# Expert weights as the stationary operand in full fp32, in place of three split fp32r products

## The reference, cut to what matters

```
def _expert_choice_ffn(h, p):
    cap = CAPACITY_FACTOR * S // N_EXPERTS            # 64 latent tokens, 16 context tokens
    aff = softmax(h @ p['w_router'] + p['b_router'])
    gate, idx = lax.top_k(aff.transpose(0, 2, 1), cap)
    xs = h[idx]                                        # the tokens of each expert
    gg, uu = xs @ w_e_gate[e], xs @ w_e_up[e]          # 1024 x 1024 each
    y = (silu(gg) * uu) @ w_e_down[e] * gate           # 1024 x 1024
    return zeros.at[idx].add(y)
```

## Time and profile before

| what | us |
|---|---|
| median of 2 runs (1469.69 to 1471.41) | 1470.55 |
| the profiled execution's own time | 1475.51 |
| its span, first to last instruction | 1473.7 |
| PE busy (share of the span) | 1327.3 (90%) |
| PEld busy | 1068.4 (72%) |
| DVE busy | 969.6 (66%) |
| ACT busy | 666.8 (45%) |
| POOL busy | 319.2 (22%) |
| HBM bytes read | 286.63 MB |

### The profile page before, as it was taken

How to read it: one execution, slowest core, us unless ns; L and a number is a source line. 1 busy time by engine, 2 the same in 40 slices (tenths; PEclk the granted TensorE clock), 3 DMA queues, 4 the chain that set the end, 5 groups by cost and what they waited for, 6 DMA issues and landing times.

```text
span 1473.7 us, 18979 instructions
## 1 busy us (share of the span) xinstructions
PE 1327.3 (90%) x7386; PEld 1068.4 (72%) x7386; DVE 969.6 (66%) x1083; ACT 666.8 (45%) x718; POOL 319.2 (22%) x199
## 2 busy tenths in 40 slices
PE   4699998899689999999979846999999999999992
PEld 3488787799568889999979734666666666666661
DVE  5443345467896643261365464999999999999993
ACT  3642232222233431241321224777777777777772
POOL 0211132000022222232322130222222222222212
PEclk9688799999799999999999757999999999999997
DMA  9645244112210112112520396999999999999974
GB/s 288 220 127 187 86 128 87 58 58 83 90 42 17 43 48 68 58 58 87 203 85 30 131 383 214 353 379 383 384 383 383 384 382 382 382 381 375 378 254 151
DMA packets 155867, 302.55 MB, mean 205 GB/s; under 512 B 6810, under 2 KB 60501, under 8 KB 155552
## 3 DMA queue, kind: packets, MB, share of 16 engines
q1 hardware_dynamic: 144268, 267.89, 50.6%
q0 software_dynamic: 3760, 12.45, 4.1%
q10 hardware_dynamic: 7782, 21.40, 4.0%
HBM read 286.63 MB, written 15.08 MB: 205 GB/s over the span
## 4 chain that ended last, share of the span: by engine, by line
PE 81%; DVE 10%; ACT 3%; DMA 2%; issue 2%; SPq 1%; POOL 0%; ACTq 0%; POOLq 0%; DVEq 0%
PE bank L1270 15%; PE bank L1271 14%; PE bank L1272 14%; PE bank L1293 5%; PE bank L1296 4%; PE bank L1294 4%; PE bank L1295 4%; PE bank L1297 4%; PE bank L1298 4%; DVE fa L899 2%; PE bank L1495 1%; PE bank L1329 1%; PE bank L1568 1%; PE bank L1330 1%; DMA wring<-in_w_ada 1%
## 5 line engine op out<-in xcount | busy, mean ns | idle before, releaser
L1202 DVE TENSOR_TENSOR l2r<-w,h2r 128x2048 fp32r<-128x2048 f32 x189 | 431.6, 2290 | 55.5 <-ACT h2r L806 53.7
L806 ACT CAST h2r<-w 128x2048 fp32r<-128x2048 f32 x192 | 367.1, 1913 | 131.4 <-PE bank L1272 128.5
L1270 PE MATMUL bank<-h2r,xTh 128*80 128x512 f32 x512 | 203.5, 397 | 1.0 <-DVE xTl L1208 1.0
L1271 PE MATMUL bank<-l2r,xTh 128*80 128x512 f32 x512 | 202.4, 395 | 0.0
L1272 PE MATMUL bank<-h2r,xTl 128*80 128x512 f32 x512 | 200.6, 392 | 0.0
L433 POOL TENSOR_TENSOR lring<-wring,hring 128x2048 fp32r<-128x2048 f32 x23 | 107.3, 4668 | 222.0 <-ACT hring L530 222.0
L489 POOL TENSOR_TENSOR half<-half 1x1 f32<-1x1 f32 x32 | 67.6, 2113 | 369.0 <-DVE ye L1246 367.7
L530 ACT CAST hring<-wring 128x2048 fp32r<-128x2048 f32 x39 | 74.3, 1907 | 104.6 <-PE bank L1298 59.0
L899 DVE SCALAR_TENSOR_TENSOR fa<-fa,cwT 128x655 f32<-128x655 f32 x120 | 110.3, 983 | 0.0
L1272 PEld LDWEIGHTS bank<-h2r,xTl 128*80 128x80 f32 x512 | 76.3, 149 | 43.2 <-issue 0.9
L1293 PE MATMUL bank<-hTh,hring 128*128 128x320 f32 x304 | 103.0, 339 | 5.0 <-DVE lring L883 5.0
(11 more groups left out here) (274 smaller groups left out, 2771.8 us busy)
## 6 DMA issues: line engine op xcount, KB each, us to landing
w<-in_w_e_gate SPq DMA_DIRECT2D x64, 1024.0 KB, 13.7
w<-in_w_e_up SPq DMA_DIRECT2D x64, 1024.0 KB, 13.8
w<-in_w_e_down SPq DMA_DIRECT2D x64, 1024.0 KB, 12.8
wring<-in_w_in SPq DMA_DIRECT2D x20, 1024.0 KB, 5.2
wring<-in_w_ada SPq DMA_DIRECT2D x12, 1024.0 KB, 6.3
fa<-in_w_ada SPq DMA_DIRECT2D x12, 1024.0 KB, 5.8
fa<-in_w_in SPq DMA_DIRECT2D x4, 1024.0 KB, 5.6
wring<-in_w_out SPq DMA_DIRECT2D x4, 1024.0 KB, 5.3
```

Of the source, the lines that this page charges most:

```text
L806: act.copy(h2r[:, k % 3, :], w2[:, k, :]).then_inc(e_hi, 1)
L1202: dve.tensor_tensor(l2r[:, k % 3, :], w2[:, k, :], h2r[:, k % 3, :].bitcast(F32), ALU.subtract).then_inc(e_lo, 1)
L1270: pe.matmul(out, lh, rh, start=start, stop=False)
L1271: pe.matmul(out, lh, rl, start=False, stop=False)
```

## The change

The weights are no longer split. A unit is now 256 rows by all 1024 columns of any of the three matrices. PE takes each 128 x 128 block of the raw fp32 unit as the stationary operand and moves the 80 token columns (`xT2` or `hT2`, fp32) past it. A unit is 8 column blocks by 2 row blocks, 16 plain fp32 matmuls. The result comes out feature-major (features on partitions, tokens along the row), so that the gated product needs no turn before `down`, but the result of `down` does: ACT copies it to `yT2` (`y_out`) and PE turns it back (`turn_back`, 8 transposes with 128 moving columns), behind the first unit of the next expert. `w2` becomes a ring of 16 units, freed by `e_unit`; SP sends 13 early, and the other three after the second norm (`s_h2`). SiLU, product and copies work on 128 x 320 tiles in place of 80 x 512. The loops are written out for all 16 experts. Gate and up units are read as two neighbouring rows per partition (8 KB in one piece), and `turn_tokens` takes every second column of `xe` to match.

```diff
-            w2 = place(p2, "w2", [P, 12, UN])
-            h2r = place(p2, "h2r", [P, 3, UN], F32R)
-            l2r = place(p2, "l2r", [P, 3, UN], F32R)
+            w2 = place(p2, "w2", [P, RING, UN])
...
-            xTh = place(p2, "xTh", [P, DC, M_E], F32R)
-            xTl = place(p2, "xTl", [P, DC, M_E], F32R)
...
+            xT2 = place(p2, "xT2", [P, DC, M_E])
+            hT2 = place(p2, "hT2", [P, DC, M_E])
+            yT2 = place(p2, "yT2", [P, DC, M_E])
...
+            for n in range(N_E * E_N):
+                e, (name, r) = n // N_E, EXPERT_UNITS[n % N_E]
+                src = a[name][0, e, 256 * r:256 * r + 256, :]
+                if n == EARLY_SLOTS:
+                    sp.wait_ge(s_h2, TT)
+                if n >= RING:
+                    sp.wait_ge(e_unit, n - RING + 1)
...
-            for k in range(3):
-                gp.wait_ge(e_hi, k + 1)
-                gp.tensor_tensor(l2r[:, k, :], w2[:, k, :], h2r[:, k, :].bitcast(F32), ALU.subtract).then_inc(e_lo, 1)
...
+            def y_out(e):
+
+                for hf in range(2):
+                    if hf == 0:
+                        act.wait_ge(e_down, e + 1)
+                    else:
+                        act.wait_ge(e_unit, N_E * e + N_E)
+                    act.copy(yT2[:, 4 * hf:4 * hf + 4, :],
+                             bank[4 + hf][:, 0:4 * M_E].rearrange("p (c t) -> p c t", c=4)).then_inc(e_yt, 1)
...
+            for e in range(E_N):
+                silu(e)
+                if e < E_N - 1:
+                    x_out(e + 1)
+                y_out(e)
...
+            def weigh(e):
+
+                if e >= 1:
+                    dve.wait_ge(e_add, 16 * e)
                 for hf in range(2):
+                    dve.wait_ge(e_yb, 2 * e + (hf + 1))
                     x = slice(512 * hf, 512 * hf + 512)
-                    dve.scalar_tensor_tensor(ye[:, x], bank[4 + hf][0:M_E, :], gateT[:, at(e)], g2r[:, x], ALU.mult,
+                    dve.scalar_tensor_tensor(ye[:, x], bank[2 + hf][0:M_E, :], gateT[:, at(e)], g2r[:, x], ALU.mult,
...
+            for e in range(E_N):
+                gated(e)
+                weigh(e)
...
+            def expert_unit(e, k):
+
+                n = N_E * e + k
+                r = k % 4
+                pe.wait_ge(e_w[n % RING], 16 * (n // RING + 1))
+                w = w2[:, n % RING, :].rearrange("p (c n) -> p c n", c=2)
+                x = hT2 if k >= 8 else xT2
+                for j in range(DC):
+                    out = bank[2 * (k // 4) + j // 4][:, M_E * (j % 4):M_E * (j % 4) + M_E]
+                    for c in range(2):
+                        last = pe.matmul(out, w[:, c, j * P:(j + 1) * P], x[:, 2 * r + c, :], start=r == 0 and c == 0 and j % 4 == 0,
+                                         stop=r == 3 and c == 1 and j % 4 == 3)
+                    if j == 3 and k == 7:
+                        last.then_inc(e_up, 1)
+                    if j == 3 and k == 11:
+                        last.then_inc(e_down, 1)
                 last.then_inc(e_unit, 1)
...
+            def turn_back(e):
+
+                for hf in range(2):
+                    pe.wait_ge(e_yt, 2 * e + (hf + 1))
+                    for c in range(4):
+                        last = pe.transpose(bank[2 + hf][0:M_E, c * P:(c + 1) * P], yT2[:, 4 * hf + c, :], ident[:, :])
+                    last.then_inc(e_yb, 1)
+
+            turn_tokens(0)
+            for e in range(E_N):
+                pe.wait_ge(e_xh, 2 * e + 2)
+                expert_unit(e, 0)
+                if e >= 1:
+                    turn_back(e - 1)
+                for k in range(1, 4):
+                    expert_unit(e, k)
+                if e >= 1:
                     pe.wait_ge(e_y, 2 * e)
+                for k in range(4, 8):
+                    expert_unit(e, k)
+                if e < E_N - 1:
+                    turn_tokens(e + 1)
+                for k in range(8, 12):
+                    if k % 2 == 0:
+                        pe.wait_ge(e_h, 2 * e + (k - 6) // 2)
+                    expert_unit(e, k)
+            turn_back(E_N - 1)
```

More of the change, by code:

```diff
@@ L96, in freed @@
     return dve, sum((JOBS[i][0] in BY_DVE) == dve for i in range(n + 1))
[L100 to L110, removed]
+EXPERT_UNITS = [("w_e_gate", r) for r in range(4)] + [("w_e_up", r) for r in range(4)]
+EXPERT_UNITS += [("w_e_down", r) for r in range(4)]
+N_E = len(EXPERT_UNITS)
+RING = 16
+EARLY_SLOTS = 13
 ITEMS = [(-1, h) for h in range(H)] + [(n, h) for n in range(4) for h in range(H)]
@@ L259, in trunk @@
         with ExitStack() as p2:
-            w2 = place(p2, "w2", [P, 12, UN])
-            h2r = place(p2, "h2r", [P, 3, UN], F32R)
-            l2r = place(p2, "l2r", [P, 3, UN], F32R)
+            w2 = place(p2, "w2", [P, RING, UN])
             xe = place(p2, "xe", [M_E, D])
-            xTh = place(p2, "xTh", [P, DC, M_E], F32R)
-            xTl = place(p2, "xTl", [P, DC, M_E], F32R)
-            sg = place(p2, "sg", [M_E, D])
-            hTh2 = place(p2, "hTh2", [P, DC, M_E], F32R)
-            hTl2 = place(p2, "hTl2", [P, DC, M_E], F32R)
+            xT2 = place(p2, "xT2", [P, DC, M_E])
+            hT2 = place(p2, "hT2", [P, DC, M_E])
+            yT2 = place(p2, "yT2", [P, DC, M_E])
             ye = place(p2, "ye", [M_E, D])
@@ L307, in trunk @@
         s_route = sem("s_route"); s_va = sem("s_va"); s_gm = sem("s_gm"); s_a2 = sem("s_a2"); s_xp = sem("s_xp"); s_u0 = sem("s_u0"); s_aa = sem("s_aa"); s_pa = sem("s_pa")
[L308 to L311, removed]
+        e_w = [sem(f"e_w{i}") for i in range(RING)]; s_bc2 = sem("s_bc2")
+        e_unit = sem("e_unit"); e_up = sem("e_up"); e_down = sem("e_down")
+        e_col = sem("e_col"); e_x = sem("e_x"); e_xt = sem("e_xt"); e_xh = sem("e_xh")
+        e_sg = sem("e_sg"); e_h = sem("e_h"); e_yt = sem("e_yt"); e_yb = sem("e_yb")
         e_y = sem("e_y"); e_cs = sem("e_cs"); e_add = sem("e_add"); s_g2 = sem("s_g2")
@@ L398, in _ @@
             unit_used(sp, N_U - 1)
[L400 to L410, removed]
+            for n in range(N_E * E_N):
[5 more added lines that the diff above has]
+                    sp.wait_ge(e_unit, n - RING + 1)
+                if name == "w_e_down":
+                    sp.dma_start(w2[:, n % RING, :].rearrange("p (c n) -> p c n", c=2),
+                                 src.rearrange("(c p) n -> p c n", p=P)).then_inc(e_w[n % RING], 16)
+                else:
+                    sp.dma_start(w2[:, n % RING, :], src.rearrange("(p c) n -> p (c n)", c=2)).then_inc(e_w[n % RING], 16)
         @block.gpsimd
@@ L497, in _ @@
             gather(0)
-            def expert(e, last):
-                if not last:
+            for e in range(E_N):
+                if e < E_N - 1:
                     gp.wait_ge(e_xt, 2 * e + 2)
                     gather(e + 1)
-                if not (isinstance(e, int) and e == 0):
+                if e >= 1:
                     gp.wait_ge(e_add, 16 * e)
@@ L510, in expert @@
                                       compute_op=ALU.add).then_inc(e_add, 16)
[L512 to L515, removed]
             for t in range(TT):
@@ L800, in _, with x_out @@
             act.dma_start(g2r[CAP_S:M_E, :], mods_d[0:1, 3 * D:4 * D].to_broadcast([CAP_P, D])).then_inc(s_g2, 16)
[L802 to L808, removed]
+            def x_out(n):
                 for hf in range(2):
                     act.wait_ge(e_xt, 2 * n + (hf + 1))
-                    act.copy(xTh[:, 4 * hf:4 * hf + 4, :],
+                    act.copy(xT2[:, 4 * hf:4 * hf + 4, :],
@@ L813, in x_hi @@
                              bank[6 + hf][:, 0:4 * M_E].rearrange("p (c t) -> p c t", c=4)).then_inc(e_xh, 1)
[L815 to L844, removed]
@@ L846, in _, with silu @@
-            for k in range(3):
-                e_hi_unit(0, k)
-            softmax_exp(TT - 1)
[L849 to L854, removed]
+            def silu(e):
+                act.wait_ge(e_unit, N_E * e + 4)
+                for hf in range(2):
+                    act.activation(hT2[:, 4 * hf:4 * hf + 4, :], bank[hf][:, 0:4 * M_E].rearrange("p (c t) -> p c t", c=4),
+                                   ACT.Silu).then_inc(e_sg, 1)
@@ new lines, in y_out @@
+            def y_out(e):
+                for hf in range(2):
+                    if hf == 0:
+                        act.wait_ge(e_down, e + 1)
+                    else:
+                        act.wait_ge(e_unit, N_E * e + N_E)
+                    act.copy(yT2[:, 4 * hf:4 * hf + 4, :],
+                             bank[4 + hf][:, 0:4 * M_E].rearrange("p (c t) -> p c t", c=4)).then_inc(e_yt, 1)
+            softmax_exp(TT - 1)
+            x_out(0)
+            for e in range(E_N):
[3 more added lines that the diff above has]
+                y_out(e)
@@ L1223, in expert, with gated @@
[L1223 to L1242, removed]
+            def gated(e):
+                for hf in range(2):
+                    if hf == 0:
```

(92 more changed lines are left out.)

17 lines of the change are left out of this document (removed).

## The result

The changed kernel takes 1679.7 us (median of 2 runs, 1678.75 to 1680.66) against 1470.55: ratio 1.142, 95% interval 1.139 to 1.145. The forecast was 1675.

The account below looks back on a forecast made before the run. TensorE was taken to bound the expert stage, DMA close behind. To 1470.6 us came +162 for pairs and turns at 2.4 GHz and +44 for the low clock: 1676, taken as 1675; range 1620 to 1800.

Parts of the forecast that it names:

- The bound: Expert stage: TensorE sets its time, DMA's floor 41 us under; taking work from DVE and ACT alone gains nothing.
- Price of a pair: Expert matmuls: weight load sets 0.1125 us a pair at 2.4 GHz, 80 columns hidden; 6144 pairs, 691.2 us.
- Turns: Expert stage, 15 of each: turn_tokens 0.55 us each, 8.3 in all; turn_back 8 x 0.11 each, 13.2 in all.
- The clock: Expert stage: 1.2 GHz through expert 0, 2.4 from its turn_back on; +44 us, chance 0.37.
- a later one: Expert stage: the clock rises only at a later turn_back burst, 41 us more an expert: 1716, 1757, 1798; chance 0.26.
- rival B: Expert stage: the clock never reaches 2.4 GHz, 2283 us; chance 0.16.
- rival C: Expert stage: the matmul stream alone raises the clock to 2.4 GHz within the first units, 1636 us; chance 0.15.
- Rival D: Expert matmuls: loads at the transposes' pace, 0.07 us a pair, DMA the bound, stage about 470 us, total 1390; chance 0.04.
- Zero prices: Expert stage: SiLU, product, copies and SP's longer queue lie beside PE's work and cost nothing.
- The sum: Expert stage: +162 us at 2.4 GHz plus 44 for the low clock, +206 in all.
- The end: Expert stage's end: ACT's last copy and 4 transposes come ahead of the second half of ye, +0.7 us.
- the token split: Expert stage's start: the split of the tokens on DVE falls away, so PE may start earlier, -0.5 us.

Follow-up runs that it names:

- e3: Changed kernel with token columns zero-padded so that 128 columns move in place of 80: 1636.4 us, ratio 1.113 to the kernel before.
- e4: Changed kernel loading only 64 of each block's 128 weight columns, half of the output features left out: 1427.0 us, ratio 0.970 to the kernel before.
- e1: Changed kernel with the 8 turn-back transposes placed singly between matmuls of units 1 and 2 of the next expert, not as one burst: 2263.8 us.
- e2: Changed kernel with 16 extra identity transposes, into a bank nobody reads, behind the first unit of expert 0: 1641.0 us.
- e7: Changed kernel with 22 matmuls of 384 fp32r columns on constants before the expert stage, during the gather: 1676.1 us, ratio 1.140 to the kernel before.
- e10: Changed kernel with gate and up units laid out like down units, so token turns load neighbouring columns: 1676.2 us, ratio 1.139 to the kernel before.
- e5: Changed kernel moving only 40 of the 80 token columns, half of the products left out: 2267.6 us.
- e8: Changed kernel with 34 warming matmuls during the gather and 6 behind the first tokens' turns: 1634.6 us, ratio 1.111 to the kernel before.
- e6: Kernel before the change with 22 warming matmuls on constants ahead of its expert stage: 1469.1 us, ratio 1.000.
- e9: Kernel before the change with 30 warming matmuls ahead of its expert stage and 6 more behind the tokens' turns: 1467.8 us, ratio 0.9986.

## Why the prediction was right

- **The bound.** TensorE set the stage before and after; the empty DVE and ACT gave nothing back. Right.
- **Price of a pair.** I took 0.1125 from plain fp32 streams with 1 and 16 columns and argued that 80 would hide behind the load. Measured 0.1115; and 128 columns (e3) and 64 loaded ones (e4) show that it is the load. At 1.2 GHz I took 0.215; 32 pairs from 976.33 to 983.15 are 0.213.
- **Turns.** `turn_back` took 0.88 us, as costed. `turn_tokens` was mis-sized, 0.94 us for 0.55, 6 us in all: the row that I took it from loads neighbouring columns, the change every second one. The cheaper pairs (6144 x 0.001 = 6 us) hid it in the sum.
- **The clock.** Cold through expert 0, up at its `turn_back`, held to the end: as forecast, near 985 us, and e1 and e2 show the burst to be the cause. This was the weakest step: it had 0.37, and that the first burst would do it, not a later one (0.26), was a guess on which 41 us hung. It was no luck of one run: the ten runs of the kernels that spend expert 0 at 1.2 GHz and keep the burst where it was (the changed kernel, e7, e10) all lie between 1672 and 1681 us, with no 1716 among them. In e5 the same burst failed, so the rise could have failed; I could not have excluded rival B, which e1 and e5 then showed in full (2264 and 2268 us against the 2283 that I gave it), nor rival C (1636), whose time e2, e3 and e8 reached by other ways (1641, 1636, 1635).
- **Rival D** needed loads at the transposes' pace. It is out as forecast, but the 0.07 that I took for that pace was misread: transposes with 128 moving columns stand 0.11 apart and those with 80 stand 0.07, in the ratio of their columns, so the 0.07 is what 80 columns stream, and of the load it says only that it is not longer. e4, which halves the load, comes to that pace and shows what lay behind it: a stage of 510 us set by DMA, where I had said 470 and had left out the gathers and adds.
- **Zero prices.** PE waited for no engine but at the start, and SP's longer queue starved nobody. Right.
- **The sum.** The stage took 756.6 us (893.25 to 1649.8) for 550.6: +206.0, where the pairs, the turns and the clock had been summed to 162 + 44. The end took the +0.7 forecast. The profiled span grew by only 203.0, since the stage began 3.7 us earlier. Of that the token split is 0.5, as forecast; most of the rest was there before the gather (issued at 885.30 in place of 888.09), and across the runs here with the changed kernel's block in front that point wanders from 880.4 to 886.1. The median lies 4.7 us above 1675. Taking off the 5.0 by which the profiled run of before stood above its median was right, for the later runs of the kernel before have medians of 1469.7 to 1471.8; it gave 1676.6, which I put down as 1675. The other 3 us are within what the block in front varies by, and no run here says more of them.

## What to carry to other kernels

Price a matmul with few moving columns by its weight load, and take the load from a stream in the trace that has almost no columns: if 1 and 16 columns stand equally far apart, so will more, as long as their own streaming time (0.067 us for 80 here, 0.107 for 128) stays under that beat. A plain fp32 matmul pays that load twice here. And ask at which clock a thin stream starts: this one held 2.4 GHz but did not reach it alone, so put dense work directly ahead of such a stream, without a gap, or pad the stream; here a pad of 48 useless columns saved 43 us, and breaking up a burst of eight transposes cost 584.

## What the runs showed of the hardware that I had not expected

- A busy TensorE can stay at 1.2 GHz for 1337 us without one idle stretch (e1; e5 with 40 columns), while the pairs of e1 hold 2.4 GHz for over 700 us (e8).
- 1.8 us of waiting ahead of eight turns, and 0.5 behind them, went before the loss of a clock that had just been won (e7); so did 0.36 and 1.26 (e6), while 0.72 ahead of the turns alone did not lose it (e9).
- Eight fp32 transposes in a row with 128 moving columns raised the clock amid the stream of 80 columns; the eight with 80 moving columns at 947.95 us did not.
- Loading every second column of a transpose's fp32 operand spaces transposes 0.117 us apart (the changed kernel), neighbouring columns 0.07 (e10).
- DMA sustained 389 GB/s over 501 us when it was the bound (e4), a little under the 395 of the earlier trace rows.
